# Two score products ahead of the second half of the value features, in a fused transformer trunk on one core

## The reference

```python
def mla(h, cos, sin, w_down, q_norm, w_uq, kv_norm, w_ukv, w_o):
    c_q, c_kv, k_rope = jnp.split(h @ w_down, [Q_LORA, Q_LORA + KV_LORA], axis=-1)
    q = (rms_norm(c_q, q_norm) @ w_uq).reshape(B, S, MLA_HEADS, QK_NOPE + QK_ROPE)
    ...
    kv = (rms_norm(c_kv, kv_norm) @ w_ukv).reshape(B, S, MLA_HEADS, QK_NOPE + V_HEAD)
    k_nope, v = kv[..., :QK_NOPE], kv[..., QK_NOPE:]
    for start in range(0, S, Q_BLOCK):
        s = (q_nope . k_nope + q_rope . k_rope) * scale      # einsum per head, blocks of 128 queries
        p = jax.nn.softmax(jnp.where(mask, s, -jnp.inf), axis=-1)
        outs.append(p @ v[:, :end])
    return o @ w_o
```

## Time and profile before

| | |
|---|---|
| median of 3 runs | 1148.28 us (1147.27 to 1151.68) |
| profiled execution, its own time | 1148.64 us |
| its span, first to last instruction | 1146.9 us |
| PE busy | 1082.3 us (94%) |
| DVE busy | 627.0 us (55%) |
| ACT busy | 522.5 us (46%) |
| mean granted TensorE clock | 0.983 |
| HBM traffic | 341.37 MB read, 299 GB/s over the span |

### The profile page before, as it was taken

How to read it: one execution, slowest core, us unless ns; L and a number is a source line. 1 busy time by engine, 2 the same in 40 slices (tenths; PEclk the granted TensorE clock), 3 DMA queues, 4 the chain that set the end, 5 groups by cost and what they waited for, 6 DMA issues and landing times.

```text
span 1146.9 us, 15627 instructions
## 1 busy us (share of the span) xinstructions
PE 1082.3 (94%) x5708; PEld 801.1 (70%) x5708; DVE 627.0 (55%) x706; ACT 522.5 (46%) x571; POOL 22.5 (2%) x94
## 2 busy tenths in 40 slices
PE   7899999999999997999998999998999998999994
PEld 7867788888799776787455787445787445787441
DVE  6755555446654448896105897105897105897102
ACT  5544444344435653775004676004676004676001
POOL 2100000000000000000000000000000000000000
PEclk9889999999999998999999999999999999999998
DMA  9932456555455331998899999999999999999994
GB/s 347 343 103 90 148 187 208 189 171 192 155 183 184 110 110 50 370 360 322 316 414 410 405 414 410 363 413 411 404 414 410 359 412 411 404 415 408 354 412 194
DMA packets 110934, 343.46 MB, mean 299 GB/s; under 512 B 11613, under 2 KB 38282, under 8 KB 100618
## 3 DMA queue, kind: packets, MB, share of 16 engines
q1 hardware_dynamic: 110714, 341.93, 78.8%
q10 hardware_dynamic: 144, 0.52, 0.1%
HBM read 341.37 MB, written 1.05 MB: 299 GB/s over the span
## 4 chain that ended last, share of the span: by engine, by line
PE 79%; DMA 7%; DVE 6%; SPq 3%; ACT 3%; issue 3%; POOL 0%; POOLq 0%; ACTq 0%; DVEq 0%
PE ps L1486 20%; PE ps L1481 19%; PE ps L1483 18%; PE ps L1482 18%; DMA raw<-moe_w_gate_up_dram 4%; SPq L369 2%; DMA raw<-moe_w_down_dram 2%; ACT whi L558 1%; DVE wlo L959 1%; PE ps L1816 1%; DVE h L1214 1%; ACT xs L558 1%; PE ps L1496 1%; DVE h L1142 1%; DVE wlo L948 0%
## 5 line engine op out<-in xcount | busy, mean ns | idle before, releaser
L558 ACT ACTIVATE whi<-raw 128x2048 fp32r<-128x2048 f32 (+1 forms) x195 | 335.8, 1724 | 241.2 <-PE ps L1483 222.5
L959 DVE TENSOR_TENSOR wlo<-raw,whi 128x2048 fp32r<-128x2048 f32 x151 | 345.3, 2291 | 120.2 <-ACT whi L558 119.1
L1481 PE MATMUL ps<-whi,xhi 128*128 128x512 f32 (+3 forms) x688 | 264.9, 385 | 18.4 <-DVE wlo L959 9.6
L1483 PE MATMUL ps<-wlo,xhi 128*128 128x512 f32 (+3 forms) x688 | 260.2, 378 | 0.0
L1482 PE MATMUL ps<-whi,xlo 128*128 128x512 f32 (+3 forms) x688 | 259.9, 378 | 0.0
L1481 PEld LDWEIGHTS ps<-whi,xhi 128*128 128x128 f32 x688 | 130.3, 189 | 47.4 <-issue 10.0
L1486 PE MATMUL ps<-raw,xs 128*64 128x512 f32 (+2 forms) x1024 | 155.0, 461 | 0.0
L1483 PEld LDWEIGHTS ps<-wlo,xhi 128*128 128x128 f32 x688 | 130.0, 189 | 24.0
L1482 PEld LDWEIGHTS ps<-whi,xlo 128*128 128x128 f32 x688 | 130.2, 189 | 22.3
L1486 PEld LDWEIGHTS ps<-raw,xs 128*64 128x64 f32 x1024 | 68.2, 137 | 81.7 <-issue 71.5
L1481 PE MATMUL ps<-whi,hhi 128*128 128x512 f32 x264 | 105.9, 401 | 0.0
(11 more groups left out here) (295 smaller groups left out, 955.7 us busy)
## 6 DMA issues: line engine op xcount, KB each, us to landing
raw<-moe_w_gate_up_dram SPq DMA_DIRECT2D x256, 512.0 KB, 12.8
raw<-moe_w_down_dram SPq DMA_DIRECT2D x80, 1024.0 KB, 17.2
raw<-moe_w_gate_up_dram SPq DMA_DIRECT2D x96, 384.0 KB, 9.4
raw<-ffn_w_gate_up_dram SPq DMA_DIRECT2D x44, 512.0 KB, 4.9
raw<-ffn_w_down_dram SPq DMA_DIRECT2D x22, 512.0 KB, 4.0
raw<-kv_shared_w_dram SPq DMA_DIRECT2D x16, 512.0 KB, 3.9
raw<-moe_w_gate_up_dram SPq DMA_DIRECT2D x32, 256.0 KB, 9.8
raw<-moe_w_down_dram SPq DMA_DIRECT2D x16, 512.0 KB, 17.7
```

Of the source, the lines that this page charges most:

```text
L558: return nc.scalar.activation(o, i, ACT.Copy, scale=scale)
L959: V.tensor_tensor(wlo[:, s, :].rearrange("p a w -> p (a w)"), raw[:, (hh // 2) % RAW, :], whi[:, s, :].bitcast(F32).rearrange("p a w -> p ...
L1481: pe.matmul(o, a_hi, b_hi, start=start, stop=False, skip_group_check=True)
L1483: return pe.matmul(o, a_hi, b_lo, start=False, stop=stop, skip_group_check=True)
```

## The change

The second half of the value features moves behind `scores(0)` and `scores(1)` on PE. On ACT and DVE its evacuation moves behind the exponentials of heads 0 and 1 (ACT), and behind the maxima of heads 0 and 1 and the normalisation of head 0 (DVE). PE's wait for `v` moves from ahead of the loop over heads to ahead of the first `outputs`. The wait for `qrT` that stood ahead of the second half is no longer needed, since `scores` already waits for it. No instruction that computes is added or removed, and no transfer is touched.

```diff
@@ ACT
             values(0)
             for hh in range(20, 22):
                 split_high(hh)
-            act.wait_ge(used, H_WO)
-            values(1)
...
             mla_exp(0)
             mla_exp(1)
+            act.wait_ge(used, H_WO)
+            values(1)
             for hd in range(HEADS):
@@ DVE
             values(0)
             for hh in range(20, 22):
                 split_low(hh)
-            dve.wait_ge(used, H_WO)
-            values(1)
...
             mla_max(0)
             mla_max(1)
             normalise(0)
+            dve.wait_ge(used, H_WO)
+            values(1)
             for hd in range(HEADS):
@@ PE
-            for g in range(2):
-                if g == 1:
-                    pe.wait_ge(qrT_ready, 2)
+            def value_features(g):
                 for c in range(TC):
                     for k in range(2):
                         hh = H_UKV + 2 * g + k
...
                 last.then_inc(used, 2)
 
+            value_features(0)
...
             scores(0)
             scores(1)
-            for c in range(TC):
-                pe.wait_ge(v_ready[c], 2)
+            value_features(1)
             for hd in range(HEADS):
...
                 if hd + 2 < HEADS:
                     scores(hd + 2)
+                if hd == 0:
+                    for c in range(TC):
+                        pe.wait_ge(v_ready[c], 2)
                 outputs(hd)
```

## The result

In the first comparison the changed kernel took 1145.6 us (median of 7 runs, 1143.68 to 1148.92), the kernel before 1150.82 us (7 runs, 1147.27 to 1152.03). The ratio is 0.9947, with a 95% interval of 0.9932 to 0.9963: 6.1 us less (1150.82 x 0.0053), between 4.3 and 7.8. The kernel before, compared with itself, came out at 0.9989 (0.9979 to 0.9999), so a bias of about 0.1% has to be allowed for in all of them. The two profiled executions stand at 1144.04 and 1148.64 us, 4.60 apart. The forecast was 1143.1, and a gain of 5.39 against the profiled execution.

What follows compares the result with a forecast made beforehand. PE, busy 94% of the span, was taken as the bound. Stall -1.32 and clock -4.07, other terms 0, gave -5.39 from 1148.64: 1143.25 us, or 1142.9 against the median, taken as 1143.1; range 1141.2 to 1146.6.

Steps and rivals of the forecast that it cites:

- PE ahead of the loop: Scores of heads 0 and 1 end 2.79 us earlier, value features at 66.83; PE's work to there unchanged: 0.
- The stall, 1.32 us: PE's idle ahead of head 0's transposes shrinks from 1.66 to 0.33 us; they start at 67.16, saving 1.32 us.
- The moved evacuations: Evacuating the second half of v later on DVE and ACT is covered before PE's first outputs: cost 0.
- The clock, 4.07 us: PE stays at 2.4 GHz from head 0's to head 2's transposes, saving 4.07 us; bounds 4.07 and 0.
- The rebuilt rounds: First two head rounds recomputed at full clock: transposes of head 1 at 71.10, of head 2 at 76.89, 5.39 us earlier.
- Later stretches: Work behind follows PE, taken as 0; the routing's clock could win 1.6 us at best or lose 2.2 at worst.
- rival 1: Stall closes but the clock falls all the same, at the new idle or old place: 1144.6 to 1147.0 us; chance 0.22.
- rival 3: Clock falls earlier, ahead of the moved value features, slowing both rounds: 1149.9 us, or 1152 with routing loss; chance 0.04.
- rival 4: No effect: head 0's exponentials not earlier, DVE being held by the weights' remainders: 1147.6 us; chance 0.04.
- Rival 2: The sum holds and the routing wins up to 1.6 us on top: 1141.3 to 1142.5 us; chance 0.15.

Runs made afterwards that it cites:

- the exchange on VectorE: Changed kernel with the second half of v evacuated ahead of head 0's normalisation on VectorE: 1147.25 us, ratio 0.9961; in a second comparison 1147.26 us, 0.9983.
- the pair of repeats: Kernel before and changed kernel, both unchanged, compared and profiled again: 1150.1 us, ratio 0.9989, and 1145.74 us, ratio 0.9955.

## Why the prediction was right

**PE ahead of the loop: nothing lost.** Right: two scores from 59.71 to 63.5, value features behind them, no pause.

**The stall, 1.32 us.** Right. With the 0.36 us by which the execution was early, the reciprocal is at 66.25 (forecast 66.28), the transposes of head 0 at 67.06 (67.16), and the idle 0.20 (0.33): 1.42 us saved in the trace. One reason that the forecast gave for the late first maximum was too simple: with the evacuation out of the way and TensorE's old order, VectorE waited for the scores of head 0 and started at 64.93 as before. Only both moves together bring it forward. Filling the stall instead and timing both kernels together fits it (0.8 us), and does not prove it.

**The moved evacuations at nothing.** Right: the copy of the probabilities ended at 67.79 and outputs started at 68.95, with a cover of 1.16 us in place of the 0.86 forecast. The forecast had laid ScalarE's operations end to end, where their records overlap by some 0.1 us each.

**The clock, 4.07 us.** Right in place and size: 13.80 - 9.77 = 4.03 us. It was shown by filling the stall without moving anything. The size was in part luck of the execution that the forecast started from: against the second profile of the kernel before it is 15.33 - 9.77 = 5.56 us. The rebuilt rounds hit each step: head 1 at 71.05 (71.10), its idle 0.87 (0.9), head 2 at 76.83 (76.89). The new idle of 0.87 did not bring the clock down in any profile here, ten profiled executions of seven kernels that have it. The Trainium skill (TensorE: Matmul & The Clock Gate, "Why this matters for your kernels") warns only of longer gaps than this stall. Read as the forecast read it, that a shorter gap does not lower the clock, it disagrees with the runs: with the stall cut from 1.66 to 0.82 us the clock held in the profiled execution.

**What I had too simple** is the reason for the fall. I put it down to the idle of 1.66 us; the exchange on VectorE brought back 1.50 us of idle and kept the clock, twice. The three profiled executions with such a stall right behind the fp32 scores (1.57 to 1.66 us) all lost the clock, and the two with 1.50 us behind the value features kept it. That the company decides fits this, and is not shown. The change takes away both the stall and the scores right ahead of it, so the forecast did not suffer.

**Later stretches at nothing, with 1.6 and 2.2 as bounds.** This is the term that was off, within its bounds. From head 2 to the end of the span the lead shrank from 5.81 to 4.6 us in the first pair of profiles, and from 6.69 (83.15 - 76.46) to 4.5 (1147.6 - 1143.1) in the pair of repeats, so 1.2 and 2.2 us were given back.

The routing, where the forecast looked for it, gave back 0.8 us in the first pair (5.94 ahead at the gather, 5.13 behind it), because the gather ran at 1.2 GHz for longer (6.33 against 5.34). This did not repeat: in the repeats the gather took 6.23 us in the changed kernel and 6.10 in the kernel before, and 0.1 was lost. So it was in the main a difference between executions. What both pairs show is a loss at the very end, which the forecast ruled out with "all work behind follows PE and moves with it": TensorE waits there for the last weight transfers, 4.0 us in sum in both profiles of the kernel before and 4.5 in both of the changed one. At the last activations ahead of these waits the lead was 5.3 and 5.6 us, behind them 4.6 and 4.5. Whether the change causes it is not shown; with other kernels here the sum of these waits lies between 3.4 and 5.3 us.

**The absolute time.** 1145.6 against 1143.1 is not a step of the sum: the kernel before stood at 1150.82 in the comparison and at 1148.28 in the three runs that the forecast started from. The gain of 6.1 us (4.3 to 7.8) holds the 5.2 to 5.4 of the forecast, and so does that of the repeat, 5.2 (1151.13 x 0.0045). The time alone does not tell the forecast from rival 1, whose 1144.6 to 1147.0 hold 1145.6 as well; the rows do.

Rival 1 (the clock falls all the same) and rival 3 (it falls earlier) are refuted by the windows at 1.00 in two profiles; rival 4 by the exponentials of head 0 at 64.76. Rival 2 (the sum, and a gain in the routing on top) is refuted as a mechanism in both pairs, since the routing won nothing; the intervals don't exclude a mean gain above the sum, which the dearer fall in the other execution of before (5.5 us) would give.

## What to carry to other kernels

Where PE is the bound, look for the places where its granted clock is down and then at what PE did before the fall: the stall in front may be short and cost little itself, and the slow stretch behind it about three times as much (1.4 us and 4.0 here). Closing the stall, in part or whole, kept the clock here; dense work beside an open stall kept it in two profiled executions, which is a lead and not a rule. Unused matmuls in it test in one run whether the clock is what it costs. A move of work between queues is one change: here PE's part alone lost 1.5 us, the other engines' part alone gave nothing, and both together gave the whole gain. And a lead won early has to be followed to the last row: here 1.2 and 2.2 us of it were gone by the end, part of it in waits for weight transfers.

## What was not expected of the hardware

The same kernel lost its clock at the same place in two profiled executions, once for 13.80 us from head 0 to head 2 and once for 15.33. The granted clock can differ between executions at the same row: the same idle of 2.4 us ahead of the first expert's transposes, in the two profiles of the changed kernel and the two of the one with the old stall in the new order, came with a fall in three of these four. A stall of 1.50 us behind matmuls of 512 columns left the clock at 1.00 where one of 1.66 behind the fp32 scores took it to 0.50; behind the same matmuls of 512 columns, 3.48 us took it down too. And a stretch in which PE counted as busy for 10.02 of 10.20 us stayed at 1.2 GHz throughout.
